# Two transformer blocks on one core: the start, the first attention and the latent attention's preparation rearranged

## The reference

```python
# first block
x = x + moba_attention(rms_norm(x, norm_mix[0]), w_qkv, w_o)   # 8 heads of 128, one block: causal
x = x + relu(rms_norm(x, norm_mlp[0]) @ up) ** 2 @ down        # 4096 wide
x = x + pool_mixer(rms_norm(x, norm_mix[1]), ...)
x = x + relu(rms_norm(x, norm_mlp[1]) @ up) ** 2 @ down
x = rms_norm(x, norm_final)
# second block, layer 0: latent attention
h = rms_norm(x, attn_pre_g[0])
cq, ckv, kr = split(h @ w_a, [384, 640])
q = rms_norm(cq, g_q) @ w_uq           # 8 heads: 128 plain, 64 rotated
k_nope, v = split(rms_norm(ckv, g_kv) @ w_ukv)
p = softmax((q_nope @ k_nope.T + rope(q_rope) @ rope(kr).T) * 192 ** -0.5 + mask)
x = x + rms_norm((p @ v) @ w_o, post_g)
x = x + rms_norm(swiglu(rms_norm(x, ...)), ...)                # 2816 wide
# layer 1: 16 heads of 64 with a table of relative biases on shared keys and values, then swiglu
```

## Time and profile before

| | us |
|---|---|
| median of 3 runs | 1194.12 (1193.29 to 1196.0) |
| the profiled execution, whole run | 1193.4 |
| its span, first to last instruction | 1191.6 |
| TensorE busy | 1132.8 (95%) |
| VectorE busy | 677.9 (57%) |
| ScalarE busy | 531.0 (45%) |
| mean granted clock of TensorE | 0.984 |

### The profile page before, as it was taken

How to read it: one execution, slowest core, us unless ns; L and a number is a source line. 1 busy time by engine, 2 the same in 40 slices (tenths; PEclk the granted TensorE clock), 3 DMA queues, 4 the chain that set the end, 5 groups by cost and what they waited for, 6 DMA issues and landing times.

```text
span 1191.6 us, 17784 instructions
## 1 busy us (share of the span) xinstructions
PE 1132.8 (95%) x7114; PEld 1008.9 (85%) x7114; DVE 677.9 (57%) x936; ACT 531.0 (45%) x644; POOL 41.9 (4%) x69
## 2 busy tenths in 40 slices
PE   4999999999999999997899999999999989999997
PEld 3887799999889999976767999999798768999996
DVE  4745644544664454466635655554765767555554
ACT  4446443443444344345434544334543664443342
POOL 0000000000000000000000000000410310000000
PEclk9999999999999999998979999999999998999999
DMA  9752446556534655544512466556754242556550
GB/s 351 254 179 69 143 157 210 166 187 202 186 104 156 206 170 187 189 128 159 177 36 71 141 188 198 177 176 224 223 177 156 86 134 72 188 177 199 176 176 35
DMA packets 127450, 196.36 MB, mean 165 GB/s; under 512 B 7393, under 2 KB 97633, under 8 KB 127281
## 3 DMA queue, kind: packets, MB, share of 16 engines
q1 hardware_dynamic: 124256, 186.29, 47.5%
q0 software_dynamic: 3152, 9.51, 2.7%
HBM read 194.73 MB, written 1.05 MB: 164 GB/s over the span
## 4 chain that ended last, share of the span: by engine, by line
PE 84%; DVE 9%; ACT 4%; issue 1%; DMA 1%; DVEq 0%; SPq 0%; ACTq 0%
PE ps L1395 26%; PE ps L1397 26%; PE ps L1396 26%; DVE wlo L895 2%; ACT whi L596 1%; DVE xs L1001 1%; ACT junk L627 1%; DMA raw<-attn_w_qkv_in 1%; PE ps L1501 1%; PE ps L1787 1%; PE ps L1785 1%; DVE act_lo L1015 1%; PE ps L1417 1%; DVE x L1046 1%; DVE xs L1042 1%
## 5 line engine op out<-in xcount | busy, mean ns | idle before, releaser
L895 DVE TENSOR_TENSOR wlo<-raw,whi 128x2048 fp32r<-128x2048 f32 (+2 forms) x173 | 389.1, 2266 | 178.9 <-ACT whi L596 177.8
L1395 PE MATMUL ps<-act_hi,whi 128*128 128x256 f32 x1384 | 392.7, 284 | 6.4 <-DVE act_lo L1015 3.4
L1396 PE MATMUL ps<-act_lo,whi 128*128 128x256 f32 x1384 | 391.7, 283 | 0.0
L1397 PE MATMUL ps<-act_hi,wlo 128*128 128x256 f32 x1384 | 391.6, 283 | 0.0
L596 ACT ACTIVATE whi<-raw 128x2048 fp32r<-128x2048 f32 (+2 forms) x172 | 321.2, 1888 | 114.1 <-PE ps L1397 99.4
L1395 PEld LDWEIGHTS ps<-act_hi,whi 128*128 128x128 f32 x1384 | 263.5, 190 | 11.3 <-issue 8.3
L1396 PEld LDWEIGHTS ps<-act_lo,whi 128*128 128x128 f32 x1384 | 263.6, 190 | 2.0
L1397 PEld LDWEIGHTS ps<-act_hi,wlo 128*128 128x128 f32 x1384 | 263.6, 190 | 0.0
L1397 PE MATMUL ps<-whi,hlo 128*128 128x512 f32 x400 | 156.8, 392 | 0.0
L1396 PE MATMUL ps<-wlo,hhi 128*128 128x512 f32 x400 | 156.8, 392 | 0.0
L1395 PE MATMUL ps<-whi,hhi 128*128 128x512 f32 x400 | 156.2, 390 | 0.0
(11 more groups left out here) (157 smaller groups left out, 889.8 us busy)
## 6 DMA issues: line engine op xcount, KB each, us to landing
raw<-mlp_w_up_in SPq DMA_DIRECT2D x32, 1024.0 KB, 6.4
raw<-mlp_w_down_in SPq DMA_DIRECT2D x32, 1024.0 KB, 4.9
raw<-ffn_w_gate_in SPq DMA_DIRECT2D x22, 1024.0 KB, 5.3
raw<-ffn_w_up_in SPq DMA_DIRECT2D x22, 1024.0 KB, 5.4
raw<-ffn_w_down_in SPq DMA_DIRECT2D x22, 1024.0 KB, 4.8
raw<-attn_w_qkv_in SPq DMA_DIRECT2D x12, 1024.0 KB, 8.6
raw<-w_kv_shared_in SPq DMA_DIRECT2D x8, 1024.0 KB, 7.0
raw<-attn_w_o_in SPq DMA_DIRECT2D x4, 1024.0 KB, 4.9
```

The lines of the kernel that those rows point to most:

```text
L895: nc.vector.tensor_tensor(wlo[:, s, 0:width], raw[:, s, 0:width], whi[:, s, 0:width].bitcast(F32), ALU.subtract).then_inc(lo_ready, 1)
L1395: nc.tensor.matmul(dst, lhsT=left[0], rhs=right[0], start=start, stop=False, **kw)
L1396: nc.tensor.matmul(dst, lhsT=left[0], rhs=right[1], start=False, stop=False, **kw)
L1397: return nc.tensor.matmul(dst, lhsT=left[1], rhs=right[0], start=False, stop=stop, **kw)
```

## The change

In the order of the program:

- Start: small constants first, then x; the first gain row is issued by ScalarE, the positions by POOL; POOL's other rows wait until the hi part of chunk 1 is made. Chunk 0 is loaded, split and multiplied in two halves. Eight small products precede the first transposes.
- The chunks of queries and keys come in the order 0, 2, 1, 3 (heads 0 to 3 first). The second half of the last value chunk (chunk 11), and the transposes of the last key heads, move into step h=2 of the first attention, their copies too (ScalarE h=2, VectorE h=3). No filler in either head loop.
- Feed-forward of the first block: the first up product goes to bank 5, the second does not wait for ReLU.
- Between the blocks: the gains of both norms are multiplied beforehand, the residual is followed at once by gains and transposes; the final norm's factor is taken in later, x itself is scaled later still. The down-projection runs by channel halves and token tiles; lora gains and transposes of the first tile stand between its last products. The query part of the lora norm is never applied to the queries: it multiplies the scores, as a factor per row in the exponential (`by_row`, `q_scale`).
- Keys of the second half of the heads (chunk 89) are made in step h=2 of the latent attention, its values in h=3; VectorE copies its half of them in h=4.
- The result is stored in four pieces. VectorE's bound before the last attention's post norm is one chunk lower.

The core of the diff, by engine (SP, POOL, ScalarE, VectorE, TensorE):

```diff
+    sp.dma_start(const[:, 0:C_CAUSAL], a["const"][:, 0:C_CAUSAL]).then_inc(const_loaded, 16)
     sp.dma_start(x[:, :, :], a["x"][0].rearrange("(t p) n -> p t n", p=P)).then_inc(x_loaded, 16)
-    first_row()
-    sp.dma_start(const[:, 0:C_CAUSAL], a["const"][:, 0:C_CAUSAL]).then_inc(const_loaded, 16)
-    load_one(0)
+    first = source("qkv", 0)
+    for h, landed in enumerate((first_half_loaded, w_loaded[SLOT[0]])):
+        sp.dma_start(raw[:, SLOT[0], h * D:(h + 1) * D].rearrange("p (k f) -> p k f", f=HALF),
+                     first[:, 2 * h:2 * h + 2]).then_inc(landed, 16)
     load_one(1)
...
+        for h in range(2):
+            sp.wait_ge(x_ready, 4 * 9 + 2 * t + h + 1)
+            cols = slice(h * HALF, (h + 1) * HALF)
+            sp.dma_start(out[0, t * P:(t + 1) * P, cols], x[:, t, cols]).then_inc(out_stored, 16)
...
+    for n, name in enumerate(("positions", "positions_2")):
+        pool.dma_start(pos_i[:, n, :], a[name].rearrange("a (t p) -> p (a t)", p=P),
+                       allow_slow_non_contiguous=True).then_inc(pos_loaded, 16)
+    pool.wait_ge(hi_ready, 2)
     for name in ROWS[1:ROW["pre1"] + 1]:
...
+                                 scale=at.scale if at.by_row is None else at.by_row[:, 0, t:t + 1],
...
+    act.dma_start(rows[:, 0, :], row_source["mix0"].partition_broadcast(P)
+                  .rearrange("q a n -> q (a n)")).then_inc(first_row_loaded, 16)
+    copy_turned("mix0", (0, 1))
+    for h, landed in enumerate((first_half_loaded, w_loaded[SLOT[0]])):
+        act.wait_ge(landed, 16)
+        nc.scalar.activation(whi[:, SLOT[0], h * D:(h + 1) * D], raw[:, SLOT[0], h * D:(h + 1) * D],
+                             ACT.Copy).then_inc(hi_ready if h else first_half_hi, 1)
+    cursor[0] = 1
+    copy_turned("mix0", (2, 3))
     hi_before(0)
...
+    for i in range(5):
+        copy_qkv(i)
+        if i >= 3:
+            copy_heads(act, i - 3)
+    copy_heads(act, 2)
+    hi_before(10)
+    def last_values(h):
+        if h == 2:
+            copy_heads(act, 3)
+            copy_qkv(5)
+    attention(moba, AT["wo"], last_values)
...
+    copy_turned("pre0")
+    hi_before(AT["wa"])
     stats("final")
...
+        act.wait_ge(x_ready, x_done("pre0", t))
+        act.wait_ge(squares, squares_after("pre0", t) - 1)
+        sum_squares("pre0", t, x[:, t, :], D)
+    root("pre0", 0)
+    root("pre0", 1)
+    hi_before(AT["wa"] + 2)
...
+    lora_squares(0)
+    copy_lora(0)
+    lora_squares(1)
+    copy_lora(1)
+    hi_before(AT["wa"] + 3)
+    act.wait_ge(var_ready, 2 * NORM["lora"] + 2)
+    nc.scalar.activation(stat[:, 2, 2 * NORM["lora"]:2 * NORM["lora"] + 2, :],
+                         stat[:, 1, 2 * NORM["lora"]:2 * NORM["lora"] + 2, :], ACT.Sqrt)\
+        .then_inc(root_ready, 2)
+    preload(ACT.Exp)
+    hi_before(AT["wa"] + 4)
+    copy_q(0)
+    copy_lora(2)
+    copy_lora(3)
+    hi_before(AT["uqr"] + 1)
+    copy_q(1)
+    copy_keys(0)
     copy_qr(act, 0)
     copy_qr(act, 1)
...
+    copy_values(0)
+    hi_before(AT["uq"] + 1)
+    def last_heads(h):
+        if h == 2:
+            copy_keys(1)
+        if h == 3:
+            copy_values(1)
+    attention(mla, AT["mwo"], last_heads)
...
+    for h, done in enumerate((first_half_lo, lo_ready)):
+        dve.wait_ge(hi_ready if h else first_half_hi, 1)
+        cols = slice(h * D, (h + 1) * D)
+        nc.vector.tensor_tensor(wlo[:, SLOT[0], cols], raw[:, SLOT[0], cols],
+                                whi[:, SLOT[0], cols].bitcast(F32), ALU.subtract).then_inc(done, 1)
+    cursor[0] = 1
+    split_turned("mix0", (2, 3))
...
+    for i in range(5):
+        copy_qkv(i)
+    lo_before(10)
+    def last_values(h):
+        if h == 3:
+            copy_qkv(5)
     dve.wait_ge(masks_loaded, 16)
...
+    attention(moba, lambda h: (causal[:, P:T], causal), AT["wo"], last_values)
     lo_before(AT["wo"] + 2)
...
+    def both_gains():
+        wait_row(dve, "final")
+        wait_row(dve, "pre0")
+        link(nc.vector.tensor_tensor(row("pre0"), row("pre0"), row("final"), ALU.mult))
+    mlp_layer(mlp[1], both_gains)
     lo_before(mlp[1].first + 31)
-    residual(mlp[1].first + 32, ACC["mlp1"], "mlp1")
...
+    residual(mlp[1].first + 32, ACC["mlp1"], "mlp1", then="pre0")
+    split_turned("pre0")
+    lo_before(AT["wa"])
     inverse_root("final", BOTH)
+    link(nc.vector.tensor_tensor(norm_stat("final", BOTH, 4), norm_stat("final", BOTH, 6),
+                                 norm_stat("final", BOTH, 6), ALU.mult))
+    link(nc.vector.tensor_scalar(norm_stat("final", BOTH, 4), norm_stat("final", BOTH, 4), 1.0 / D, None,
+                                 ALU.mult))
     for p in range(4):
...
+        nc.vector.tensor_tensor(x[:, t, cols], x[:, t, cols], row("final")[:, cols], ALU.mult)\
+            .then_inc(x_ready, 1)
+    dve.wait_ge(x_ready, 4 * XR["pre0"] + 4)
+    dve.sem_inc(row_used, 2)
+    mean_square("pre0", 0, before="final")
+    mean_square("pre0", 1, before="final")
...
+        inverse_root("pre0", t, mean=False, before="final")
+    lo_before(AT["wa"] + 2)
+    def lora_gained(t):
+        nc.vector.tensor_tensor(xs[:, t, 0:QL + KVL], lora_acc(t, 0, QL + KVL), row("lora", 0, QL + KVL),
+                                ALU.mult)
         k0 = QL + KVL
...
+    lo_before(AT["wa"] + 3)
+    dve.wait_ge(root_ready, 2 * NORM["lora"] + 2)
+    link(nc.vector.reciprocal(lora_stat(3), lora_stat(2)))
+    link(nc.vector.tensor_tensor(lora_stat(4), lora_stat(3), lora_stat(3), ALU.mult))
+    link(nc.vector.tensor_tensor(lora_stat(5), lora_stat(4), lora_stat(1), ALU.mult))
+    link(nc.vector.tensor_scalar(lora_stat(5), lora_stat(5), -0.5, 1.5, ALU.mult, ALU.add))
+    link(nc.vector.tensor_tensor(lora_stat(5), lora_stat(5), lora_stat(3), ALU.mult))
...
+    k0 = QL + KVL
+    for t in range(TT):
+        nc.vector.tensor_scalar(xs[:, t, QL:k0], xs[:, t, QL:k0], norm_stat("lora", t, 6, 1, 2), None,
+                                ALU.mult)
+        nc.vector.tensor_scalar(xs[:, t, k0 + 64:k0 + 128], xs[:, t, k0:k0 + 64], norm_stat("pre0", t, 6),
+                                None, ALU.mult)
+        link(nc.vector.tensor_scalar(xs[:, t, k0:k0 + 64], xs[:, t, k0:k0 + 64], norm_stat("pre0", t, 6),
+                                     None, ALU.mult))
+        dve.sem_inc(xs_ready, 1)
+    nc.vector.tensor_scalar(q_scale[:, 0, :], norm_stat("lora", BOTH, 6), mla.scale, None, ALU.mult)
+    link(nc.vector.tensor_scalar(q_scale[:, 1, :], norm_stat("lora", BOTH, 6), -mla.scale, None, ALU.mult))
...
+    rope_queries(0)
+    lo_before(AT["wa"] + 4)
+    split_lora(2)
+    split_lora(3)
+    rope_queries(1)
+    dve.sem_inc(qr_roped, 1)
+    lo_before(AT["uqr"] + 1)
     for t in range(TT):
...
+        link(nc.vector.tensor_scalar(x[:, t, :], x[:, t, :], norm_stat("final", t, 6), None, ALU.mult))
...
+    def copy_values(j):
+        dve.wait_ge(w_used, AT["ukv"] + j + 1)
+        nc.vector.tensor_copy(V[:, 1, j * HALF:(j + 1) * HALF], bank((7, 3)[j])).then_inc(v_copied, 1)
+    copy_values(0)
     lo_before(AT["uq"] + 1)
...
+    def last_heads(h):
+        if h == 4:
+            copy_values(1)
+    attention(mla, lambda h: (chunked[:, P:T], chunked), AT["mwo"], last_heads)
     lo_before(AT["mwo"] + 2)
     post("post0", None, "fpre0")
...
-    BUSY = {"mlp1": (2, 3, 3, 2, 1), "pre0": (9, 1, 1, 1, 1), "mlp0": (0, 1, 1, 0, 1),
+    BUSY = {"mlp1": (2, 3, 3, 2, 1), "pre0": (4, 1, 0, 0, 0), "mlp0": (0, 1, 1, 0, 1),
             "fpre0": (4, 1, 6, 1, 2), "kvsrc": (8, 1, 6, 1, 2), 
             "fpre1": (4, 1, 6, 1, 2),
-            moba: (0, 0, 2, 7), mla: (0, 0, 2, 1)}
+            moba: (0, 0, 0, 0), mla: (0, 0, 0, 0)}
...
+        def up(c, i, value, first=False, second=False):
             wait_chunk(value)
-            if not first:
+            if not first and not second:
                 pe.wait_ge(f.act_done, i)
...
+    def last_values(h):
+        if h == 2:
+            turn_heads(3)
+            qkv_products(5, 1)
+            pe.wait_ge(heads_copied, 8)
+        if h == 4:
+            pe.wait_ge(qkv_a, 6)
+            pe.wait_ge(qkv_v, 6)
...
+        for j in (2 * half, 2 * half + 1):
             c = AT["wa"] + j
             wait_chunk(c + 1)
...
             for k in range(2):
...
+                for lo, hi in ((0, 352), (352, 704)):
+                    ins = product(lora_acc(t, lo, hi), acts(2 * j + k, t * P, (t + 1) * P),
                                   cols(slot(c), k * 704 + lo, k * 704 + hi),
                                   start=j == 0 and k == 0, stop=j == 3 and k == 1, skip_group_check=True)
             if t == 1:
                 ins.then_inc(w_used, 1)
...
+            if n == 3 and j == 2:
+                turn_lora(0)
+        if n < 2:
+            turn("pre0", parts=(2 + n,))
+        if n == 2:
             ins.then_inc(acc_wa, 1)
...
+    def queries_of(t, k):
+        return product(bank(t), acts(k, t * P, (t + 1) * P),
```

(39 more changed lines are left out.)

431 lines of the change are left out of this document (207 added, 224 removed).

## The result

The changed kernel takes 1180.38 us in the median of 4 runs (1179.10 to 1181.23), beside 1195.06 for the kernel before, timed on the same chip: ratio 0.9877, 95% interval 0.9864 to 0.9890. That is 14.7 us less; my sum had 7.0. The runs of the kernel before that stand beside the experiments took 1192.9 to 1193.8 us where their mean granted clock was 0.984 and 1194.6 to 1196.7 where it was 0.979, so up to 3 us of a difference of medians hang on which of them it is taken against.

A forecast was written before the change was run, and what follows sets the result against it. TensorE bounds the long stages; only the start, first attention and latent surroundings can move. 6.9 - 4.0 + 0.8 + 3.0 + 0.3 = 7.0 us gained: run 1186.4, median 1187.1, range 1183 to 1191, chance 0.50.

The forecast's parts named there:

- Start: First 20 us: first product at 12.4 instead of 19.35, a gain of 6.9 us, bounds 5 and 7.7.
- bytes ahead of the gains: 1.1 MB + 0.5 MB: Start: at 327 GB/s 5 us, with some 2 us before data flows; x and row at 7.0.
- First attention: Moving 24 products behind the first scores gains nothing at full clock; with clock 4.0 us lost, bounds 0 and 7.
- the term for the clock: First attention: low clock into output products; chain +1.9 us, output products at 0.427 instead of 0.227 +2.1, 4.0 lost.
- Feed-forward: First block: second up product no longer waits for ReLU's copy, the 0.78 us pause goes; gain 0.8, 0 to 0.8.
- Latent: Latent preparation and heads: first output product 608.6 against 615.12, 6.5 gained, clock costs 3.5; net 3.0, bounds 8 and -1.
- The tail: End: last store of 256 KB instead of 512 KB, gain 0.3 us, 0 to 0.6.
- A: Rival: clock holds through both new pause groups, gain 14.5, 1179.6; chance 0.15. As distance: chunk 9's end to first output product.
- B: Rival: conversions hold nothing up, gain 25, 1169; chance 0.12. As distance: first attention's first output product to the latent one's.
- C: Rival: low clock lasts 13.6 us at both attentions, start at its bound of 5; gain about 0, 1194; chance 0.15.
- D: Rival: without filler the clock stays low while heads run; slower, up to 1208, at the middle 1199; chance 0.08.
- my three signs of being wrong: First product after 14.5, first attention gaining more than 2 us, or pause ahead of lora's transposes below 5.

The follow-up runs named there:

- experiment 6: Changed kernel with the first gain row issued by SyncE behind x instead of by ScalarE; 1181.20 us, ratio 0.9886, one outlier run left out of the ratio.
- 10: Changed kernel with the first gain row on SyncE's queue behind x and twelve instead of eight filler products at the start; 1180.88 us, ratio 0.9884.
- experiment 12: The kernel of experiment 11 with seven more filler products between the transposes of x and the first product; 1155.34 us, ratio 0.9676.
- experiment 5: Changed kernel, but SyncE waits until x has landed before issuing chunk 0's other half and chunks 1 to 3; 1180.71 us, ratio 0.9888.
- experiment 1: Changed kernel with all six query/key/value tiles again ahead of the first attention's heads and filler at steps 2 and 3 back; 1182.32 us, ratio 0.9903.
- experiments 2: Changed kernel with ScalarE and VectorE converting chunk 15 one head step later in the first attention; 1176.35 us, ratio 0.9844.
- experiments 3: Changed kernel with latent chunks 91 to 93 converted from head step 3 on by ScalarE, step 4 on by VectorE; 1175.77 us, ratio 0.9838.
- experiment 9: Changed kernel with keys and values of the last four latent heads (chunk 89) made before the heads again; 1181.57 us, ratio 0.9879.
- experiment 11: Experiment 8 with the start of 10 and a finer order of conversions, gains and squares around the latent down-projection; 1156.20 us, ratio 0.9676.
- experiment 8: Changed kernel with chunks 15, 91 to 93 later, tile 0's gains first, chunk 85 before tile 1's gains, last latent values copied at step 3; 1162.96 us, ratio 0.9742.
- experiment 4: Changed kernel with tile 0's lora gains ahead of x's products and the next norm's statistics in the latent down-projection; 1176.31 us, ratio 0.9848.

## Why the prediction was right in sign and short in size

The sum gave 1187.1 and its own range was 1183 to 1191; the 1180.4 measured lie below it, and inside 1177 to 1195 only because two rivals were taken in there. Of the sum's 7.0 us against 12.2 in the traces, the start was 1.5 too much, the first attention 3.7, the latent part 2.8 and the tail 0.2 too little.

**Start: forecast -6.9 (bounds -5 to -7.7), measured -5.4 at chunk 9's end.** Two errors of opposite sign. The first product came at 15.42, not 12.4, outside my own line of 14.5 for "wrong". The failed step is "bytes ahead of the gains: 1.1 MB + 0.5 MB ... I take x and row at 7.0". With the row on a queue of its own x took 8.3 us and landed at 9.5; with the row behind it on SyncE's queue it took 5.2 to 5.8 us (experiments 6 and 10 to 12), about the 5.3 of before. So the row's share of the wire is shown. That the chunks right behind x take a share too is not: they stand behind it in all these runs, and experiment 5 moves its landing by 0.3 us beyond what it does by itself. Nor was 7.0 in reach for the two together: where the row follows x on one queue it landed at 8.2 to 8.6. The rule I weighed (the Trainium skill, DMA: Bandwidth & Descriptors, "Issuing engines are not separate DMA queues") was right in that the row's queue brought no time (1180.38 us with it, 1181.20 in experiment 6); but I had used it only for bytes ahead, and experiment 6 shows the other side of it, that a transfer from a second issuer takes its share from x and the constants. What I left out gave 1.5 us back: before ran its first 3.15 us of products at 0.427, after ran them at 0.227. 3.9 and 1.5 make the 5.4. Those 1.5 us were luck: I had not counted on them, and two of the seven profiled runs with this start didn't have them.

**First attention: forecast +4.0, measured +0.3.** The pauses were read right in the main: 3.0, 0.8, 1.8 and 1.0 forecast, 3.03, 1.51 and 0.46 found, that of 0.8 not at all. "Nothing gained at full clock" holds (experiment 1: 0.4). What failed is the term for the clock: it did halve at 89.0, but for 3.5 us only, over score and transposes that lay beside VectorE's work, and it was full again when the first output product ran. I had it last until 4 or 5 us into the output products, from the earlier trace rows.

**Feed-forward: forecast -0.8, and that pause is gone.** B holds it.

**Latent: forecast -3.0, measured -5.8** (B fell by 6.6, less the 0.8). The pauses: 1.6 forecast and 1.70 found, 10.4 and 9.93, 5.6 and 5.04. On my frame shifted by what lies ahead (-5.9) the first score was due at 578.6 and came at 577.5. From there to the first output product I had 24.1 us at full clock and 27.6 with the clock's loss; it was 25.9. So of the 2.8 us beyond the forecast 1.1 are the preparation's and 1.7 lie in the heads, 0.6 of them because the pause was 5.0 and not 5.6, the rest the clock's, again counted too dear: low from 594.2 to 604.5, but for a third of that stretch TensorE was idle.

**The tail: forecast -0.3.** From the latent part's first output product to the end it was 576.5 us before and is 576.0: -0.5. The landing of the last store accounts for it by its size (2.6 us before, 2.1 now), but this stretch is 575.5 to 576.9 long in the other traces, so the 0.5 can't be told from none.

**Rivals.** A, "the clock holds", gave 1179.6 and is the nearest in time, yet the clock did not hold: it fell at both places and cost little. B, "everything hides", was right on what the moves can be worth (5.5 and 5 us) and wrong on this code: experiments 2 and 3 got amounts of that size only by taking the conversions out of the way. C and D fall: in the changed kernel's trace no low stage was longer than 10.5 us, and the clock came back amid the heads. (D's middle, 1199, is not the middle of 1187.1 and 1208, which is 1197.7; nothing hangs on it.) Of my three signs of being wrong one came true, the first product after 14.5; the first attention gained nothing, and the pause ahead of lora's transposes was 9.93.

**What the change's parts bring, then.** Its two moves of products into the heads are worth 0.4 and -0.4 us by the traces of experiments 1 and 9, no more than like traces differ by, although they are its name. The gain is the start (5.4), the feed-forward pause (0.8) and, by what is left over, the new order of the latent preparation with the filler gone (5.8), which the moves' experiments leave untouched. 5.4 + 0.8 + 5.8, less the 0.3 that A grew, are 11.7 of the 12.2 us between the traces. No run puts the start or the preparation back by itself, so these two shares are distances in two traces and not undone one by one.

## What to carry to other kernels

Where work is moved into a stretch to fill gaps, write down for each engine what is queued ahead of the copies that the moved work's consumers wait for; a conversion that merely may run there can cost exactly what the move earned, and letting it wait a step or two paid 4 to 5 us in each of two places. Look at what is on the wire beside what is needed first: a row of 512 KB issued by another engine at the same time made x land 1.5 to 3.2 us later, while loads issued behind it on its own queue were not seen to. And price a low clock only over the time in which the slowed engine sets the pace.

## What the runs showed that I had not expected

The clock at the start is not fixed by the code: of seven profiled runs with one and the same start, five had the first products at 0.227 us each and two at 0.427, 1.2 to 2.4 us apart at chunk 9's end; the three with the row on SyncE's queue ahead of experiment 12 all had low ones, experiment 11 only from the fifth product on. Nor does a pause's length sort the cases: the clock stayed full behind 1.70, 1.73 and 1.85 us (after, experiments 3 and 1) and behind 2.18 and 2.54 (experiment 8), and fell behind 2.32 (experiment 4) and 3.03. It also fell with nothing above 0.88 us in experiment 9: TensorE was busy for 5.53 of the 6.0 us from 586 to 592 at full clock, with the heads' short products, and for 11.70 of the 12.0 from 594 to 606 at 0.50. What exactly the clock follows stays open.
